# Weight tiles loaded as two DMAs of half the columns, each with its own semaphore

## The chip, the cores and the metric

The kernel runs on one core of one Trainium2 chip. The metric is the device time of one execution in microseconds (us), the median of several runs.

## What is computed

The reference runs one activation `x` of 256 tokens by 1024 features, all float32, through two blocks of two layers each. Every layer is a feed-forward part (FFN), a token mixer and a second FFN, each with a norm before or after it and a residual. Cut to what matters here:

```python
def swiglu(h, w_gate, w_up, w_down):          # D_MODEL 1024, D_FF 2816
    return (jax.nn.silu(h @ w_gate) * (h @ w_up)) @ w_down

for l in range(DEPTH):                        # first block, DEPTH = 2
    x = x + 0.5 * rmsnorm(swiglu(rmsnorm(x, ...), gate, up, down), ...)
    x = x + rmsnorm(hybrid_mixer(rmsnorm(x, ...), w_in, w_out, ...), ...)
    x = x + 0.5 * rmsnorm(swiglu(rmsnorm(x, ...), gate, up, down), ...)
...
for l in range(DEPTH):                        # second block: layer norms, and a
    mod = cond @ w_ada[l] + b_ada[l]          # modulation from the vector c
    ...                                       # FFN, token mixer, FFN again
```

So there are eight FFNs and four mixers. The weights, some 330 MB of gate, up, down, `w_in`, `w_out` tiles and the 72 MB of `w_ada`, are each read once from HBM.

## The kernel before

**Weight tiles and units.** Gate, up, down, `w_in` and `w_out` are laid out in HBM as tiles of 128 partitions by 2048 float32 columns, 1 MB, each partition's 8 KB in one piece. A tile goes by one DMA into one of four slots of `raw` in SBUF. A tile is worked off as two *units* of 1024 columns. For each unit ScalarE (ACT) copies the columns, rounded to fp32r, into `w_hi` (`hi_unit`, line 186), VectorE (DVE) subtracts that from `raw` and so makes the rest `w_lo` (`lo_unit`, line 192), and TensorE (PE) multiplies both parts with the two-part activation. `w_hi` and `w_lo` have three buffers.

**The semaphores of a unit.** `raw_in[slot]` counts the DMAs that landed in a slot (16 per DMA). `hi_unit` waits for it only at the first unit of a tile (`half == 0`), and always for `unit_done`, by which PE frees the buffer. `unit_hi` and `unit_lo` count finished splits; PE waits for both, and SyncE (SP) waits for `unit_lo` before it sends a new tile into a slot. `CREDIT` is a constant offset of `unit_lo` and `unit_done`.

**The FFN.** Eleven blocks (`NF`) of 256 hidden columns. In iteration i of the loop over 1 to 10 PE does two gate units, two up units (`wide_unit`, lines 225 and 230, each 8 matmuls of 512 columns and 8 of 256), and then the two down units of block i-1 (`row_unit`, lines 259 and 265, 8 matmuls and 4). Slot 0 holds gate, slot 1 up, slot 2 down. SP issues (`ffn_sp`, line 275) the gate tile as soon as the up tile before it has been split, and the up tile and the down tile together once the down tile before them has been split. In six of the eight FFNs eight of the iterations also carry a 1.5 MB chunk of `w_ada` on the same queue (line 1554). After the loop comes the **tail**: SP waits until every unit but the last two is split, issues the last down tile into slot 2, and ACT, DVE and PE do, in this order, `hi_unit`, `split_act` (line 330) and `hi_unit` on ACT; `lo_unit`, `rest_act` (line 369) and `lo_unit` on DVE; `row_unit` twice on PE. The last activation is put in `hT` here, and PE's first matmul of the tail waits for both its parts and for the first unit. Then the post norm reads the accumulators (DVE line 529 in the first block, line 555 in the second).

**The mixers.** `mixer_load` (line 592) sends the tiles of `w_in` and `w_out` into the four slots in turn, each when the tile four before it has been split; one tile of the first block's mixers is `w_small` with 160 columns, which is a single unit.

All order is written by hand: each engine's program is a list of instructions and waits.

Of the kernel before, what the change touches and what calls it, by code (L numbers as in the profile page):

```python
# [40 lines left out]
SLOTS = 4  # L41
UNIT = 1024
# [65 lines left out]
def build(nc, t, out):  # L108
    ctx = ExitStack()

    def sb(name, shape, dt=F32):
        return ctx.enter_context(nc.sbuf_tensor(name, shape, dt))

    def sem(name):
        return ctx.enter_context(nc.semaphore(name))
# [10 lines left out]
    raw = sb("raw", [P, SLOTS, KT * FB])  # L126
# [20 lines left out]
    settled = sem("settled")  # L147
    rows_in = [sem("rows_in0"), sem("rows_in1")]
    zero_set = sem("zero_set")
    raw_in = [sem(f"raw_in{i}") for i in range(SLOTS)]  # L150
    unit_hi, unit_lo = sem("unit_hi"), sem("unit_lo")
    unit_done = sem("unit_done")
    silu_done, act_ready = sem("silu_done"), sem("act_ready")
# [26 lines left out]

    def hi_unit(a, B, j, buf, slot, loads, half, width=UNIT):

        if half == 0:
            a.wait_ge(raw_in[slot], loads * 16)
        a.wait_ge(unit_done, B + (j - UBUF + 1 + CREDIT if not isinstance(j, tuple) else j[0] + (j[1] - UBUF + 1 + CREDIT)))
        nc.scalar.activation(w_hi[:, buf, 0:width], raw[:, slot, half * UNIT:half * UNIT + width],  # L186
                             ACT.Copy).then_inc(unit_hi, 1)
# [84 lines left out]

    def ffn_sp(sp, B, loads, l, wg, wu, wd, between=None):
        def load(slot, w, i):
            sp.dma_start(raw[:, slot, :], w[bass.ds(l, 1), i, :, :].rearrange("l i p n -> p (l i n)")).then_inc(
                raw_in[slot], 16)


        sp.wait_ge(unit_lo, B + (CREDIT - 6))
        load(0, wg, slice(0, 1))  # L280
        sp.wait_ge(unit_lo, B + (CREDIT - 4))
        load(1, wu, slice(0, 1))
        for first, end in FFN_LOOPS if between else ((1, NF),):
            with sp.Fori(first, end) as i:
                sp.wait_ge(unit_lo, B + i * 6 + (CREDIT - 4))
                load(0, wg, bass.ds(i, 1))
                sp.wait_ge(unit_lo, B + i * 6 + (CREDIT - 2))
                load(1, wu, bass.ds(i, 1))
                load(2, wd, bass.ds(i - 1, 1))
                if between and first == 1:  # L290
                    between(first_chunk)
                if between and first == 2:
                    between(i - 1)
        sp.wait_ge(unit_lo, B + (6 * NF - 2 + CREDIT))
        load(2, wd, slice(NF - 1, NF))
# [30 lines left out]
    def ffn_act(a, B, loads, f):  # L326
# [18 lines left out]
        for r in range(4):  # L345
            hi_unit(a, B, r if r >= UBUF - 1 else UBUF - 1, r % UBUF, r // 2, loads + 1, r % 2)
# [3 lines left out]
        with a.Fori(1, NF) as i:  # L350
            for r in range(2):
                hi_unit(a, B, (i * 6, r - 2), (r - 2) % UBUF, 0, loads + i + 1, r)
            split_act(f * NF + i - 1, B + i * 6 + (CREDIT - 2))
            for r in range(2, 4):
                hi_unit(a, B, (i * 6, r - 2), (r - 2) % UBUF, 1, loads + i + 1, r - 2)
            gate_copy(f * NF + i, B + i * 6 + CREDIT)
            hi_unit(a, B, (i * 6, 2), 2, 2, loads + i, 0)
            silu(f * NF + i)
            hi_unit(a, B, (i * 6, 3), 0, 2, loads + i, 1)
            up_copy(f * NF + i, B + i * 6 + (2 + CREDIT))  # L360
# [228 lines left out]
    def mixer_load(sp, B, ends, n, src, width=KT * FB):  # L589

        sp.wait_ge(unit_lo, B + (CREDIT + (ends[n - SLOTS] if n >= SLOTS else (-4, -2, 0, 0)[n])))
        sp.dma_start(raw[:, n % SLOTS, 0:width], src).then_inc(raw_in[n % SLOTS], 16)

    def mixer_units(ends, n):

# [164 lines left out]
    def mixer1_sp(sp, B, l):  # L760
        at = 0
        for n in range(IN1 + WO):
            if n == SMALL_AT:
                mixer_load(sp, B, ENDS1, n, t["w_small"][bass.ds(l, 1), :, :].rearrange("l p n -> p (l n)"), KT * SMALL)
            elif n < IN1:
                mixer_load(sp, B, ENDS1, n, t["w_in"][bass.ds(l, 1), at:at + 1, :, :].rearrange("l i p n -> p (l i n)"))
                at += 1
            else:
                mixer_load(sp, B, ENDS1, n,
                           t["w_out"][bass.ds(l, 1), n - IN1:n - IN1 + 1, :, :].rearrange("l i p n -> p (l i n)"))  # L770
# [747 lines left out]
    half = m2.take(TILES, 512)  # L1518
# [647 lines left out]
```

## Time and profile before

| | |
|---|---|
| median of 3 runs | 2555.84 us (2554.86 to 2558.20) |
| the profiled execution | 2557.87 us, of which its span 2556.1 us |
| PE busy | 2299.2 us, 90% of the span |
| DVE busy | 1635.9 us, 64% |
| ACT busy | 1146.8 us, 45% |
| DMA queue of SP | 444.40 MB, packets take 45.4% of 16 DMA engines' span |

The span is the time from the first to the last instruction in the profile; 1.8 us of the execution lie around it. A busy share is an average over the eight FFNs, the four mixers and the norms between them, which have different limits. The profile also gives, for any stretch, the clock that TensorE was granted (1.00 stands for 2.4 GHz, 0.50 for 1.2 GHz, and what lies between is a mix of the two within the stretch).

### The profile page before, as it was taken

The page shows a single profiled execution, that of the slowest core. Times are in us where ns is not written, and L with a number is a line of the kernel's source. Part 1 is how long each engine was busy: PE and PEld are TensorE (multiplying, and loading weights), DVE is VectorE, ACT ScalarE, POOL GpSimd, SP SyncE. Part 2 cuts the span into 40 slices and gives each one's busy share as a digit, 9 for nine tenths or more (in the row PEclk, how much of TensorE's full clock was granted, in tenths as well). Part 3 has the DMA queues.
Part 4 walks back from the last instruction along what each step waited for, and adds up shares of the span by engine and source line. Part 5 has one row for each costly group of instructions (what it writes and reads, how often), then busy time and mean ns, then how long its engine had stood idle before and what let it go on. Part 6 is the DMA issues. An engine that isn't in the chain of part 4 may idle for free. (4 is left out here: it accounts for less than half of the span.)

```text
span 2556.1 us, 36360 instructions
## 1 busy us (share of the span) xinstructions
PE 2299.2 (90%) x13308; PEld 2036.2 (80%) x13308; DVE 1635.9 (64%) x1802; ACT 1146.8 (45%) x1418; POOL 24.5 (1%) x14
## 2 busy tenths in 40 slices
PE   6998997799799989888998998967998998877996
PEld 5888897688688889777887887956887887866885
DVE  5775756577577557646765776556775665555655
ACT  4543533454455444335544553434553544443553
POOL 0000000000000000000000000000000000000000
PEclk9997997899899989889998998979998999978998
DMA  7763320276377432205755763513763444421442
GB/s 275 287 238 133 116 99 17 108 289 261 148 290 285 176 115 102 81 17 222 283 201 199 279 266 132 190 42 141 278 254 128 185 183 178 149 83 66 183 181 113
DMA packets 58954, 445.62 MB, mean 174 GB/s; under 512 B 6896, under 2 KB 7280, under 8 KB 8304
## 3 DMA queue, kind: packets, MB, share of 16 engines
q1 hardware_dynamic: 58864, 444.40, 45.4%
q8 instruction: 59, 0.97, 0.2%
q14 instruction: 31, 0.25, 0.0%
HBM read 443.33 MB, written 1.05 MB: 174 GB/s over the span
## 5 line engine op out<-in xcount | busy, mean ns | idle before, releaser
L192 DVE TENSOR_TENSOR w_lo<-raw,w_hi 128x1024 fp32r<-128x1024 f32 x670 | 811.0, 1222 | 406.6 <-ACT w_hi L186 405.6
L186 ACT ACTIVATE w_hi<-raw 128x1024 fp32r<-128x1024 f32 x670 | 702.2, 1053 | 449.4 <-PE ps L230 161.0
L225 PE MATMUL ps<-hT,w_hi 128*128 128x512 f32 x2816 | 704.7, 392 | 22.8 <-ACT w_hi L186 13.1
L225 PEld LDWEIGHTS ps<-hT,w_hi 128*128 128x128 f32 x2816 | 510.7, 189 | 123.3 <-ACT w_hi L186 18.5
L230 PEld LDWEIGHTS ps<-hT,w_lo 128*128 128x128 f32 x2816 | 384.1, 190 | 27.5
L230 PE MATMUL ps<-hT,w_lo 128*128 128x256 f32 x2816 | 392.6, 282 | 0.0
L259 PE MATMUL ps<-w_hi,act_hi 128*128 128x512 f32 x640 | 198.5, 391 | 0.0
L259 PE MATMUL ps<-w_hi,act_lo 128*128 128x512 f32 x640 | 197.6, 390 | 0.0
L265 PE MATMUL ps<-w_lo,act_hi 128*128 128x512 f32 x640 | 171.0, 389 | 0.0
L242 PE MATMUL ps<-w_hi,hT 128*128 128x256 f32 (+1 forms) x576 | 146.9, 291 | 4.7 <-DVE hT L506 4.7
L243 PE MATMUL ps<-w_hi,hT 128*128 128x256 f32 (+1 forms) x576 | 145.3, 288 | 0.0
L1568 DVE SCALAR_TENSOR_TENSOR arena<-arena,cond 128x3072 f32<-128x3072 f32 x42 | 143.4, 3413 | 0.0
L259 PEld LDWEIGHTS ps<-w_hi,act_lo 128*128 128x128 f32 x640 | 120.1, 188 | 26.2
L265 PEld LDWEIGHTS ps<-w_lo,act_hi 128*128 128x128 f32 x640 | 120.1, 188 | 24.9
L259 PE MATMUL ps<-w_hi,hT 128*128 128x512 f32 x384 | 110.8, 437 | 29.1 <-DVE hT L369 17.4
L259 PEld LDWEIGHTS ps<-w_hi,act_hi 128*128 128x128 f32 x640 | 115.1, 189 | 19.3
L452 PE MATMUL ps<-base,tok 128*128 128x128 f32 x192 | 44.0, 423 | 92.8 <-DVE tok L490 54.8
L380 DVE TENSOR_TENSOR hidden<-ps,arena 128x512 f32<-128x512 f32 x88 | 60.9, 692 | 103.0 <-ACT arena L335 103.0
L343 ACT ACTIVATE arena<-ps 128x512 f32<-128x512 f32 x88 | 52.8, 600 | 162.4 <-PE ps L230 162.4
L259 PEld LDWEIGHTS ps<-w_hi,hT 128*128 128x128 f32 x384 | 80.1, 212 | 51.6 <-DVE hT L435 13.3
L335 ACT ACTIVATE arena<-ps 128x512 f32<-128x512 f32 x88 | 52.6, 598 | 152.7 <-PE ps L230 152.7
L242 PEld LDWEIGHTS ps<-w_hi,hT 128*128 128x128 f32 x576 | 114.2, 198 | 7.4 <-DVE hT L506 5.5
(314 smaller groups left out, 2656.6 us busy)
## 6 DMA issues: line engine op xcount, KB each, us to landing
raw<-in_g SPq DMA_DIRECT2D x88, 1024.0 KB, 4.8
raw<-in_u SPq DMA_DIRECT2D x88, 1024.0 KB, 4.8
raw<-in_d SPq DMA_DIRECT2D x88, 1024.0 KB, 6.7
arena<-in_w_ada SPq DMA_DIRECT2D x48, 1536.0 KB, 7.5
raw<-in_w_in SPq DMA_DIRECT2D x54, 1024.0 KB, 4.8
raw<-in_w_out SPq DMA_DIRECT2D x16, 1024.0 KB, 4.8
rows<-in_rows SPq DMA_DIRECT2D x12, 1024.0 KB, 6.8
arena<-in_con SPq DMA_DIRECT2D x1, 1344.0 KB, 5.7
```

Source lines behind the costliest of these rows:

```text
L186: nc.scalar.activation(w_hi[:, buf, 0:width], raw[:, slot, half * UNIT:half * UNIT + width], ACT.Copy).then_inc(unit_hi, 1)
L192: nc.vector.tensor_tensor(w_lo[:, buf, 0:width], raw[:, slot, half * UNIT:half * UNIT + width], w_hi[:, buf, 0:width].bitcast(F32), ALU.su ...
L225: nc.tensor.matmul(o, h_[:, k, c], hT[:, :, 4 * half + k, :], start=(half == k == 0), stop=False)
L230: last = nc.tensor.matmul(ps[:, bank + s, 0:SEQ], l_[:, k, c], hT_hi[:, 4 * half + k, :], start=False, stop=(half == 1 and k == 3))
L242: nc.tensor.matmul(o, hT_hi[:, 4 * half + k, c], h_[:, k, :], start=(half == tile == k == 0), stop=False)
L243: nc.tensor.matmul(o, hT_lo[:, 4 * half + k, c], h_[:, k, :], start=False, stop=False)
L259: nc.tensor.matmul(ps[:, 2 * tile + half, :], part[:, c], w_hi[:, buf, half * 512:(half + 1) * 512], start=start and i == 0, stop=False)
L265: last = nc.tensor.matmul(ps[:, 2 * tile + half, :], left[0][:, c], w_lo[:, buf, half * 512:(half + 1) * 512], start=False, stop=stop)
L335: nc.scalar.activation(part, ps[:, 4:6, SEQ:512], ACT.Copy).then_inc(gate_part, 1)
L343: nc.scalar.activation(part, ps[:, 6:8, SEQ:512], ACT.Copy).then_inc(up_part, 1)
L380: nc.vector.tensor_tensor(out_, in_, part, ALU.add).then_inc(gate_sum, 1)
L1568: nc.vector.scalar_tensor_tensor(ada, ada_w, cond[:, bass.ds(k, 1)], ada, ALU.mult, ALU.add).then_inc(ada_acc, 1)
```

## The change

Every load of a weight tile is issued as two DMAs, the first for the left half of the columns, the second for the right half. Each half has its own semaphore per slot, and `hi_unit` now waits for the semaphore of its own half, in both units. The narrow unit of `w_small`, whose two halves are both read by the one unit, waits for both.

```diff
-    raw_in = [sem(f"raw_in{i}") for i in range(SLOTS)]
+    raw_in = [[sem(f"raw_in{i}{h}") for h in "ab"] for i in range(SLOTS)]
...
     def hi_unit(a, B, j, buf, slot, loads, half, width=UNIT):
 
-        if half == 0:
-            a.wait_ge(raw_in[slot], loads * 16)
+        a.wait_ge(raw_in[slot][half], loads * 16)
+        if width < UNIT:
+            a.wait_ge(raw_in[slot][1], loads * 16)
...
     def ffn_sp(sp, B, loads, l, wg, wu, wd, between=None):
         def load(slot, w, i):
-            sp.dma_start(raw[:, slot, :], w[bass.ds(l, 1), i, :, :].rearrange("l i p n -> p (l i n)")).then_inc(
-                raw_in[slot], 16)
+            for half in range(2):
+                c = slice(half * UNIT, (half + 1) * UNIT)
+                sp.dma_start(raw[:, slot, c], w[bass.ds(l, 1), i, :, c].rearrange("l i p n -> p (l i n)")).then_inc(
+                    raw_in[slot][half], 16)
...
     def mixer_load(sp, B, ends, n, src, width=KT * FB):
 
         sp.wait_ge(unit_lo, B + (CREDIT + (ends[n - SLOTS] if n >= SLOTS else (-4, -2, 0, 0)[n])))
-        sp.dma_start(raw[:, n % SLOTS, 0:width], src).then_inc(raw_in[n % SLOTS], 16)
+        for half in range(2):
+            c = slice(half * width // 2, (half + 1) * width // 2)
+            sp.dma_start(raw[:, n % SLOTS, c], src[:, c]).then_inc(raw_in[n % SLOTS][half], 16)
```

On ACT, in the FFN's tail, these are the rows before: the last down tile's two splits around `split_act`. The names are the tiles written and read, and in brackets the semaphores waited for.

```order
L184 ISA
L185 REGISTER_ALU [waits raw_in2]
L186 ACTIVATE w_hi<-raw 128x1024 [waits unit_done]
L328 REGISTER_ALU
L330 ACTIVATE hT<-hidden 128x512 [waits unit_done,act_ready]
L185 REGISTER_ALU
L186 ACTIVATE w_hi<-raw 128x1024 [waits unit_done]
```

And these in the changed kernel:

```order
L183 ISA
L186 REGISTER_ALU [waits raw_in2a]
L187 ACTIVATE w_hi<-raw 128x1024 [waits unit_done]
L331 REGISTER_ALU
L333 ACTIVATE hT<-hidden 128x512 [waits unit_done,act_ready]
L186 REGISTER_ALU [waits raw_in2b]
L187 ACTIVATE w_hi<-raw 128x1024 [waits unit_done]
```

The number and order of the instructions are the same; the second split's wait rides on a register instruction that was there before.

On SP, at the end of the loop and in the tail, before:

```order
L287 REGISTER_ALU
L275 DMA raw<-in_u 128x2048 [waits unit_lo]
L275 ISA
L275 DMA raw<-in_d 128x2048
L284 REGISTER_ALU
L284 COMPARE_AND_BRANCH
L294 REGISTER_ALU
L275 ISA [waits unit_lo]
L275 DMA raw<-in_d 128x2048
```

And in the changed kernel:

```order
L290 REGISTER_ALU
L278 DMA raw<-in_u 128x1024 [waits unit_lo]
L278 DMA raw<-in_u 128x1024
L278 ISA
L278 DMA raw<-in_d 128x1024
L278 ISA
L278 DMA raw<-in_d 128x1024
L287 REGISTER_ALU
L287 COMPARE_AND_BRANCH
L297 REGISTER_ALU
L278 ISA [waits unit_lo]
L278 DMA raw<-in_d 128x1024
L278 ISA
L278 DMA raw<-in_d 128x1024
```

Each DMA became two, one behind the other under the same wait; nothing else moved.

## Rows read from the trace of the kernel before

**Rows 1.** The page, part 1: busy us (share of the span) xinstructions.

```profile
PE 2299.2 (90%) x13308; PEld 2036.2 (80%) x13308; DVE 1635.9 (64%) x1802; ACT 1146.8 (45%) x1418; POOL 24.5 (1%) x14
```

**Rows 2.** Waits of ACT: us in total, times, longest us.

```profile
ACT w_hi L186 <- DMA raw<-in_d: 31.3, 8, 4.4
...
ACT w_hi L186 <- DMA raw<-in_u: 0.4, 1, 0.4
```

**Rows 3.** Timeline, last FFN's tail: start us, us, engine line op [idle before].

```profile
2523.61 0.34 SPq L275 DMA_DIRECT2D raw<-in_d  x1
...
2528.41 1.07 PE L265 MATMUL ps<-w_lo,act_hi 128*128 128x512 f32 x4
2528.43 1.06 ACT L186 ACTIVATE w_hi<-raw 128x1024 fp32r<-128x1024 f32 x1 [3.78 <-DMA raw<-in_d]
2529.40 0.61 ACT L330 ACTIVATE hT<-hidden 128x512 fp32r<-128x512 f32 x1
2529.52 1.23 DVE L192 TENSOR_TENSOR w_lo<-raw,w_hi 128x1024 fp32r<-128x1024 f32 x1 [3.29 <-ACT w_hi L186]
...
2530.67 0.68 DVE L369 TENSOR_TENSOR hT<-hidden,hT 128x512 fp32r<-128x512 f32 x1
...
2531.45 2.48 PE L259 MATMUL ps<-w_hi,hT 128*128 128x512 f32 x8 [1.97 <-DVE hT L369]
...
2538.85 2.35 DVE L555 TENSOR_TENSOR tok<-ps,arena 128x1024 f32<-128x1024 f32 x2 [6.37 <-PE ps L265]
```

**Rows 4.** Timeline, PE and DVE in the tails of the first and fifth FFN.

```profile
205.41 3.49 PE L259 MATMUL ps<-w_hi,hT 128*128 128x512 f32 x8 [2.73 <-DVE hT L369]
...
1558.52 2.08 PE L259 MATMUL ps<-w_hi,hT 128*128 128x512 f32 x8 [1.94 <-DVE hT L369]
...
1564.27 2.35 DVE L555 TENSOR_TENSOR tok<-ps,arena 128x1024 f32<-128x1024 f32 x2 [4.71 <-PE ps L265]
```

**Rows 5.** Windows: from:to us, engines' busy times, PEclk, DMA share, GB/s.

```profile
205.40:209.00 3.60, 3.59 (x10) 2.88 (x11) 0.91 (x1) 0.00 (x0) 0.00 (x0) 0.58 0.56 178
1558.50:1562.00 3.50, 3.48 (x15) 2.92 (x16) 1.06 (x1) 0.83 (x1) 0.00 (x0) 1.00 0.67 232
2531.40:2535.00 3.60, 3.55 (x11) 2.85 (x12) 1.08 (x1) 0.85 (x1) 0.00 (x0) 0.71 0.00 0
```

**Rows 6.** Timeline, PE at the start of the first FFN.

```profile
23.18 2.11 PE L225 MATMUL ps<-hT,w_hi 128*128 128x512 f32 x8 [1.59 <-DVE hT L506]
```

**Rows 7.** DMA issues by line: xcount, KB each, median us from issue to landing.

```profile
raw<-in_u SPq DMA_DIRECT2D x88, 1024.0 KB, 4.8
raw<-in_d SPq DMA_DIRECT2D x88, 1024.0 KB, 6.7
arena<-in_w_ada SPq DMA_DIRECT2D x48, 1536.0 KB, 7.5
...
x<-in_x SPq DMA_DIRECT2D x1, 1024.0 KB, 5.2
...
base<-in_con SPq DMA_DIRECT2D x1, 256.0 KB, 5.3
raw<-in_w_small SPq DMA_DIRECT2D x2, 80.0 KB, 1.8
```

**Rows 8.** Timeline of the queue of SP: the kernel's first two loads.

```profile
0.75 0.45 SPq L1885 DMA_DIRECT2D x<-in_x  x1
...
1.25 0.46 SPq L1886 DMA_DIRECT2D base<-in_con  x1
```

**Rows 9.** Timeline, one loop iteration of the last FFN, SP and ACT.

```profile
2407.31 0.33 SPq L275 DMA_DIRECT2D raw<-in_u  x1
...
2407.86 0.33 SPq L275 DMA_DIRECT2D raw<-in_d  x1
...
2413.76 1.04 ACT L186 ACTIVATE w_hi<-raw 128x1024 fp32r<-128x1024 f32 x1
...
2423.93 0.33 SPq L275 DMA_DIRECT2D raw<-in_u  x1
```

## The prediction, made before the changed kernel ran

> **What bounds the kernel now.** The page's first part shows PE busy for 90% of the span [rows 1], so time can only be won where PE stands idle or runs at a low clock. A load can matter only where a split waits for it. The waits of ACT, read next, say where that is: the split at line 186 waited for a down tile 8 times, 31.3 us in total, and once, for 0.4 us, for an up tile; it never waited for a gate tile or for a tile of the mixers [rows 2]. There are eight FFNs, and the 8 waits are the eight tails. Everywhere else the tile has landed before ACT wants it. One loop iteration shows the margin: an up tile issued at 2407.31 lands 4.8 us later [rows 7], at 2412.11, and its first split starts at 2413.76 [rows 9], 1.65 us after that. So the loops and the mixers are bound by PE, and only the tails by a load.
>
> The timeline of a tail gives the chain [rows 3]. SP issues the last down tile at 2523.61, and the first split starts when it has landed, at 2528.43, 4.82 us later. Then the activation's split (2529.40 to 2530.01) and, on DVE, `w_lo` (2529.52 to 2530.75) and the activation's rest at line 369 (2530.67 to 2531.35), and PE starts at 2531.45. From the landing to PE's start that is 3.02 us of fixed work. PE had finished its earlier matmuls at 2529.48 and stood idle for 1.97 us. The other tails are alike, PE idle for 1.94 to 2.73 us [rows 3, 4]; five more lie between the three shown.
>
> That idle time costs a second time. In the last tail it takes 7.40 us from PE's first matmul (2531.45) to the post norm's first read of the result (2538.85) [rows 3], in the fifth FFN 5.75 us (1558.52 to 1564.27) [rows 4], for the same instructions. The granted clock explains it: 0.71 in the last tail's first 3.6 us and 0.58 in the first's, but 1.00 in the fifth's [rows 5]; the eight matmuls at line 259 take 3.49 us in the first tail and 2.08 us in the fifth [rows 4]. In seven of the eight tails the clock falls to the 1.2 GHz level for some 3 us just after the gap. In the last tail that costs 7.40 - 5.75 = 1.65 us, in the first 3.49 - 2.08 = 1.41 us; of the six tails between them in the timeline the fifth loses nothing and the other five 1.62 to 1.66 us each. Together 1.65 + 1.41 + 5 x 1.64 = 11.3 us.
>
> **The change, part by part.** *The first half lands earlier.* This is the term that counts, and no row shows a load of 512 KB alone, so I bound it. An up tile lands 4.8 us after its issue; the down tile issued 0.55 us later lands 6.7 us after its own, which is 2.45 us after the up tile [rows 7, 9]. So 1 MB takes the queue 2.45 us, and 4.8 - 2.45 = 2.35 us are paid once. With the queue's rate alone, half a tile lands at 2.35 + 1.23 = 3.58 us, 1.22 us earlier than now. The other bound is the line between `w_small` (80 KB in 1.8 us) and the full tile (1024 KB in 4.8 us) [rows 7]: 1.8 + 432 x 3.0 / 944 = 3.17 us, 1.63 us earlier. I take the middle, rounded down: 1.4 us. The chain behind it is on ACT, DVE and PE and does not change; its other inputs are ready (the activation was, PE's buffer too, since ACT's one wait of 3.78 us ended at the DMA [rows 3]). PE is idle for at least 1.94 us, so the whole 1.4 us reaches it: 8 x 1.4 = **11.2 us**.
>
> *The second half* is issued some 0.4 us behind the first (0.33 us for the issue and a register instruction) and lands about when the tile lands now, at 4.8 to 5.2 us. It is wanted by the second split, which stands behind the first (landing at 3.4, plus 1.06) and behind the activation's split (0.61), at 5.1 us. Even if it is 0.3 us late, PE needs that unit only after the first unit's 2.8 us of matmuls. Cost nothing, hidden by PE's first unit.
>
> *The clock.* With 1.4 us less of idle time, PE's gap in the tails shrinks from 1.94-2.73 to 0.5-1.3 us. At the eight FFN starts PE stands idle for up to 1.59 us just before its first matmuls, and these then run at full speed: 2.11 us for 8, as in the tail that kept its clock [rows 4, 6]. So I expect the clock to hold in the tails, and **11.3 us** to come back. The bounds are 0 (it still falls in seven) and 11.3.
>
> *ACT's added waits*: no instruction is added, the wait for the second half rides on one that stood there. What is queued behind it is ACT's next split and the activation's, and PE behind them. In the loop the second half is wanted 2.2 us after the first, and the first had 1.65 us to spare: nothing. *SP's added issues*: a tile costs SP one more issue of 0.33 us. In the loop three tiles go in 16.62 us (2407.31 to 2423.93 [rows 9]), so SP has the time; the down tile, issued behind the up tile, comes some 0.4 us later and the `w_ada` chunk 0.7 us later, each long before use. *Twice as many and smaller pieces*: 4 KB instead of 8 KB per partition, strided in HBM. Near rows: `x`, in pieces of 4 KB, lands at 0.75 + 5.2 = 5.95, and `base`, 256 KB in strided pieces of 2 KB, at 1.25 + 5.3 = 6.55 [rows 7, 8]. That is 0.60 us for 256 KB, or 2.4 us per MB, no worse than the 2.45 of the 8 KB pieces. Nothing. The mixers gain nothing: no split there waits for a load.
>
> The profiled execution is 2557.87 us, its span 2556.1 and 1.8 us around it. From it the sum is 2557.9 - 11.2 - 11.3 = 2535.4. It stood 2.0 us above the median of the runs, so the forecast for the median is 2555.8 - 22.5 = **2533.3 us**.
>
> *A page against a row.* The rows put 2.35 us of fixed time in a load and 1.22 to 1.63 us into half of a tile's bytes [rows 7, 9]. The Trainium skill, "DMA: Bandwidth & Descriptors", section "Anatomy of one DMA — SWDGE (gpsimd) path", fits 2.0 us plus the bytes over 436e3; half a tile would by that land 1.2 us earlier, and the first term would be an estimated 9.6 us in place of 11.2.
>
> **The rivals.** *The clock still falls.* The smaller gap may not be small enough, or the falls may depend on more than the gap: 1.94 us of idle kept the clock and 1.97 lost it [rows 3, 4]. For it: that thin edge. Against: gaps of up to 1.59 us that lose nothing [rows 6]. Then only the landing counts: 2555.8 - 11.2 = 2544.6 us.
>
> *The first half does not come earlier*, because the two halves share the queue and finish together, so that the change doesn't do what it says. Against it: the up tile lands at 4.8 us although the down tile is queued 0.55 us behind it, so the queue works in order [rows 7, 9]. For it: two DMAs 0.4 us apart could overlap more than two 0.55 us apart. Then the first split starts as now or up to 0.4 us later: 2555.8 to 2559.
>
> *Slower: each DMA pays its fixed part in turn.* If two halves do not overlap, a tile holds the queue for 2 x 3.58 = 7.2 us. An iteration of 16.62 us brings three tiles, in 48 of the 80 iterations also a chunk of 1.5 MB (1.5 x 2.45 = 3.7 us) [rows 7, 9]. Then 3 x 7.2 = 21.5 us bind the loop, 4.9 us too long in all 80 and 3.7 more in the 48: 390 + 178, or some 3110 us with the tails' gain. It decides from (16.62 - 3.7) / 3 = 4.3 us per tile; the rows have 2.45. The Trainium skill, same page, section "Measured (HBM→SBUF, 128 partitions, SWDGE, issued from GpSimd)", has the rule behind this, to batch DMAs to 1 MiB or more; the trace's back-to-back loads speak against it here, since the second lands 2.45 us after the first.
>
> **How the numbers follow.** The forecast 0.62; the clock still falls 0.20; no earlier half 0.12; slower loops 0.04; the rest, 0.02, for a larger gain. The range takes in the first two: at the low end 8 x 1.63 + 11.3 = 24.3 us gained, and at the high end 8 x 1.22 = 9.8 us and no clock, 2531.5 to 2546.0. The kernel's clock falls in many other places too, each fall being worth about 1.6 us, and their number may shift with the timing; I add 3.5 to 4 us each side: 2528 to 2550. A measurement of this kernel can tell about 0.2% (5.1 us) from no change. Faster by more: the first two cases and the rest, less a little for an unlucky clock, 0.82. Same: 0.13. Slower: 0.05.
>
> **What would show it.** In the waits, the line of ACT on the down tile should fall from 31.3 us to about 31.3 - 11.2 = 20. In the tails the first split should start 3.2 to 3.6 us after the issue, PE's gap should be 0.5 to 1.3 us, and the time from PE's first matmul to the post norm 5.75 us, with a granted clock of 1.00. The loop should still take 16.62 us, and two tiles in a row still land 2.4 to 2.5 us apart. It is wrong if the first half lands at 4.5 us or later, if the clock in the tails is still near 0.6, or if ACT begins to wait for loads inside the loop.

## The result, and the profile after

The changed kernel takes 2540.81 us (median of 4 runs, 2537.62 to 2542.17) against 2556.35 us for the kernel before (4 runs): 15.5 us less, a ratio of 0.9937 with a 95% interval of 0.992 to 0.9954. Timed a second time it was 17.0 us less (2538.47 against 2555.50 us), a ratio of 0.9929 (0.9911 to 0.9946). The forecast was faster, by 22.5 us. The direction held; the size forecast was 7 us too large.

The page of the profiled execution (2542.17 us, span 2540.3), its engines, its queue and its loads, to be read beside [rows 1] and [rows 7]:

```profile
PE 2293.6 (90%) x13308; PEld 2032.6 (80%) x13308; DVE 1636.4 (64%) x1802; ACT 1146.3 (45%) x1418; POOL 24.5 (1%) x14
...
q1 hardware_dynamic: 107248, 444.42, 49.8%
...
raw<-in_g SPq DMA_DIRECT2D x176, 512.0 KB, 4.6
raw<-in_u SPq DMA_DIRECT2D x176, 512.0 KB, 4.7
raw<-in_d SPq DMA_DIRECT2D x176, 512.0 KB, 6.6
arena<-in_w_ada SPq DMA_DIRECT2D x48, 1536.0 KB, 9.1
```

The work is the same. The queue's packets take 49.8% of the span in place of 45.4%, and a chunk of `w_ada`, which stands behind the halves, lands 9.1 us after its issue, 7.5 before [rows 7]. So the halves are not free for the queue. The waits of ACT say whether that matters:

```profile
ACT w_hi L187 <- PE ps L231: 162.0, 168, 1.8
...
ACT w_hi L187 <- DMA raw<-in_d: 24.1, 8, 3.4
```

There are still exactly 8 waits for a down tile, the eight tails; those for other tiles are gone. But the 8 fell only from 31.3 us [rows 2] to 24.1, by 0.9 us each, where 1.4 was forecast. The last FFN's tail, which answers to [rows 3]:

```profile
2510.35 1.03 SPq L278 DMA_DIRECT2D raw<-in_d  x2
...
2514.27 1.06 ACT L187 ACTIVATE w_hi<-raw 128x1024 fp32r<-128x1024 f32 x1 [2.88 <-DMA raw<-in_d]
...
2515.15 1.07 PE L266 MATMUL ps<-w_lo,act_hi 128*128 128x512 f32 x4
...
2515.95 1.06 ACT L187 ACTIVATE w_hi<-raw 128x1024 fp32r<-128x1024 f32 x1
...
2517.30 2.06 PE L260 MATMUL ps<-w_hi,hT 128*128 128x512 f32 x8 [1.07 <-issue]
...
2523.02 2.36 DVE L558 TENSOR_TENSOR tok<-ps,arena 128x1024 f32<-128x1024 f32 x2 [4.69 <-PE ps L266]
```

The first split starts 3.92 us after the issue (4.82 before; 3.8 to 4.3 in all eight tails), PE's gap is 2517.30 - 2516.22 = 1.08 us (1.97 before), the 8 matmuls take 2.06 us (2.48), and from PE's first matmul to the post norm it is 5.72 us (7.40). The clock held. In windows of the last and the first tail, to be read beside [rows 5], the column PEclk stands at 1.00 where it was 0.71 and 0.58:

```profile
204.10:207.70 3.60, 3.56 (x16) 2.96 (x17) 0.94 (x1) 0.00 (x0) 0.00 (x0) 1.00 0.93 340
2517.30:2520.90 3.60, 3.60 (x16) 3.01 (x17) 1.03 (x1) 1.01 (x1) 0.00 (x0) 1.00 0.00 0
```

All eight tails are so. From the tile's issue to the post norm's first read, the eight tails took 120.8 us before and 102.9 us after: 17.9 us less, of which 11.2 are the clock (57.2 us from PE's first matmul to the post norm before, 46.0 after) and 6.7 the landing. (Measured by PE's gaps, 17.4 us in all before and 10.2 after, the landing gives 7.2, because in two of the tails the issue itself comes 0.1 and 0.4 us sooner, seen from PE's earlier work.) The spans differ by 15.8 us, so elsewhere the kernel was 2.1 us *longer*. Whether the halves cost that was the first open question; the second was why half a tile comes only 0.9 us earlier.

### The profile page after: what moved, and what is told of

It is laid out like the page before. It is cut to its first block and busy times, and to the rows that moved or that the text cites. A ratio compares the mean times of both kernels' runs of the same rounds, so it can differ in the third digit from the quotient of the medians.

```text
span 2540.3 us, 37230 instructions
## 1 busy us (share of the span) xinstructions
PE 2293.6 (90%) x13308; PEld 2032.6 (80%) x13308; DVE 1636.4 (64%) x1802; ACT 1146.3 (45%) x1418; POOL 24.5 (1%) x14
## 3 DMA queue, kind: packets, MB, share of 16 engines
q1 hardware_dynamic: 107248, 444.42, 49.8%
## 5 line engine op out<-in xcount | busy, mean ns | idle before, releaser
L226 PEld LDWEIGHTS ps<-hT,w_hi 128*128 128x128 f32 x2816 | 510.7, 189 | 122.9 <-ACT w_hi L187 18.4
L260 PE MATMUL ps<-w_hi,hT 128*128 128x512 f32 x384 | 103.0, 413 | 21.9 <-DVE hT L438 11.8
L243 PEld LDWEIGHTS ps<-w_hi,hT 128*128 128x128 f32 x576 | 115.1, 200 | 7.4 <-DVE hT L509 5.5
L244 PEld LDWEIGHTS ps<-w_hi,hT 128*128 128x128 f32 x576 | 115.2, 200 | 0.0
```

The lines of the kernel that those rows point to most:

```text
L226: nc.tensor.matmul(o, h_[:, k, c], hT[:, :, 4 * half + k, :], start=(half == k == 0), stop=False)
L243: nc.tensor.matmul(o, hT_hi[:, 4 * half + k, c], h_[:, k, :], start=(half == tile == k == 0), stop=False)
L244: nc.tensor.matmul(o, hT_lo[:, 4 * half + k, c], h_[:, k, :], start=False, stop=False)
L260: nc.tensor.matmul(ps[:, 2 * tile + half, :], part[:, c], w_hi[:, buf, half * 512:(half + 1) * 512], start=start and i == 0, stop=False)
```

## How the experiments are read

The kernel's time moves by several us between executions that are otherwise alike (the kernel before gave 2543 to 2561 us over all runs). The traces show where. I cut each trace at two points of each FFN that every kernel has: the start of the last product of gate and up on DVE, from which the tail's work hangs, and the post norm's first read. The sum of the eight pieces between them is "tails", the rest up to the last tail "between". "Tails" holds the clock's part and the change of PE's gaps, 11.2 + 7.2 = 18.4 us for the change. All in us, one profiled execution each:

| kernel | tails | between | time against before, with interval |
|---|---|---|---|
| before | 106.1 | 2432.8 | 1 |
| the change | 87.7 | 2435.4 | 0.9937 (0.992 to 0.9954) |
| the change, again | 87.4 | 2432.7 | 0.9929 (0.9911 to 0.9946) |
| halves in the tails alone | 87.8 | 2429.3 | 0.9945 (0.9923 to 0.9967) |
| halves everywhere but in the tails | 103.3 | 2435.0 | 1.0009 (0.9994 to 1.0024) |
| tails' gap filled on PE | 94.7 | 2430.9 | 0.9972 (0.9959 to 0.9985) |
| last down tile in slot 3 | 75.3 | 2432.8 | 0.9885 (0.9859 to 0.9912) |
| slot 3, again | 75.3 | 2437.6 | 0.988 (0.9865 to 0.9895) |
| one DMA of 4 KB pieces | 105.5 | 2431.2 | one execution, no interval: 2555.65 us |
| second half sent after the first | 85.4 | 2431.3 | one execution, no interval: 2535.87 us |
| each half in one piece of HBM | 82.6 | 2435.7 | one execution, no interval: 2537.42 us |
| the same, timed | 82.9 | 2426.0 | 0.9899 (0.9881 to 0.9917) |

"Tails" repeats within 0.3 us for a like kernel. "Between" runs from 2426 to 2438 with no order in it that the edits would give.

## Experiments: where the gain is made

**Halves in the tails alone.** The kernel before, with this in place of the last down load, and a wait for `tail_in` at the last split:

```diff
-        load(2, wd, slice(NF - 1, NF))
+        for half in range(2):
+            c = slice(half * UNIT, (half + 1) * UNIT)
+            sp.dma_start(raw[:, 2, c], wd[..., NF - 1:NF, :, c]...).then_inc(tail_in if half else raw_in[2], 16)
```

> The kernel before, with only the last down tile of each FFN loaded as two halves; every other tile goes by one DMA as before. Theory: the whole gain of the change (15.5 us) is made in the eight tails, where the traces show 17.9 us less from the tile's issue to the post norm, and the twice as many DMAs in the loops and mixers do nothing. Then about 2540.8 us, as the change, with the tail's first split starting 3.8 to 4.3 us after the issue. Rival: the small DMAs in loops and mixers cost the 2 us that are missing between 17.9 and 15.8; then about 2538.5 us.

Measured: 2537.59 us, ratio 0.9945. The eight halved loads of the tails bring what halving all of them brought. The waits of ACT are those of the change, 24.1 us there:

```profile
ACT w_hi L189 <- DMA raw<-in_d: 24.2, 8, 3.5
```

**The change again, and its complement.** The second kernel is the change with the tail's tile whole again:

```diff
+        sp.dma_start(raw[:, 2, :], wd[..., NF - 1:NF, :, :]...).then_inc(raw_in[2][0], 16)
...
         hi_unit(a, B, 6 * NF - 2, (6 * NF - 2) % UBUF, 2, loads + NF, 0)
+        a.sem_inc(raw_in[2][1], 16)
```

> The changed kernel again, beside the two that follow. Theory: 15 to 16 us under the kernel before, of which the tails' landing gives 6.6 and their clock the rest. Rival (the halves in loops and mixers cost time): it stays slower than the kernel with halves in the tails alone (5.5 permille under before in the job ahead) by 2 us or more.

> The changed kernel, but the last down tile of each FFN is again one DMA of 1 MB. Theory: the halves in loops and mixers are hidden by PE's work, both ways, so this is the kernel before: no difference above 0.1% (2 to 3 us). Rival: they cost about 2 us (the traces of before and after differ by 2.1 us in that sense outside the tails), a ratio of 1.001.

Measured: 0.9929 and 1.0009. The change is not behind the kernel that halves only the tails (0.9929 and 0.9945, intervals overlapping), and halves in all loops and mixers but not in the tails are no different from the kernel before; the interval leaves room for a cost of up to 0.24% and for none. The gain is made in the tails. The 2.1 us that were missing between the first two traces are within the scatter of "between" and I don't put them down to the DMAs.

## Experiments: the clock

**PE's gap filled.** The loads are those of before; PE does six matmuls of zeros in front of the tail:

```diff
+        pe.wait_ge(act_ready, f * NF + (NF + 1))
+        for _ in range(6):
+            nc.tensor.matmul(ps[:, 6, :], zero[:, 0:P], zero[:], start=True, stop=True)
         pe.wait_ge(act_split, f * NF + NF)
```

> The kernel before, loads unchanged, but PE does six matmuls of zeros (128 x 512, bf16, into a PSUM bank that is free there) between its last loop unit and the tail, about 1.8 us that fill most of its gap of 1.94 to 2.73 us. Theory: the clock falls in the tails because PE stands idle there; filled, it holds, each tail takes 5.75 us from PE's first useful matmul to the post norm, and the kernel gains 11.3 us: about 2545 us. Rival: the falls don't hang on the gap (or zeros don't count as work): still 7.4 us per tail, 2556 us.

Measured: 2546.05 us, ratio 0.9972. The last tail and its window, columns as above:

```profile
2516.86 1.06 ACT L186 ACTIVATE w_hi<-raw 128x1024 fp32r<-128x1024 f32 x1 [3.77 <-DMA raw<-in_d]
...
2517.98 1.24 PE L322 MATMUL ps<-zero 128*128 128x512 bf16 x5
...
2519.88 2.09 PE L259 MATMUL ps<-w_hi,hT 128*128 128x512 f32 x8 [0.66 <-issue]
...
2525.64 1.23 DVE L558 TENSOR_TENSOR tok<-ps,arena 128x1024 f32<-128x1024 f32 x1 [4.72 <-PE ps L265]
```

```profile
2519.50:2523.00 3.50, 3.12 (x14) 2.60 (x15) 1.41 (x2) 1.18 (x1) 0.00 (x0) 1.00 0.00 0
```

ACT still waits 3.77 us for the tile, PE's useful work starts as late as before, and yet each tail is 5.76 to 5.79 us from there to the post norm: the eight sum up to 11.4 us less than before. With nothing changed but what PE does in the gap, the clock's fall is gone, so the gap causes it. (The row of zeros has five of the six matmuls; one record is missing. They leave 0.57 to 1.36 us of idle time.) The timed gain is smaller than the trace's 11.4, 7 us (4 to 10). The next rows give a part of the reason: a kernel with a whole tile in the tail doesn't always lose seven tails. These are two tails of the kernel with halves everywhere but in the tails:

```profile
1561.36 3.65 PE L260 MATMUL ps<-w_hi,hT 128*128 128x512 f32 x8 [1.93 <-DVE hT L374]
...
2156.76 2.09 PE L260 MATMUL ps<-w_hi,hT 128*128 128x512 f32 x8 [1.93 <-DVE hT L374]
```

The same gap of 1.93 us lost the clock once and kept it once. In the three traces with a whole tile in the tail the clock fell in 7, 6 and 5 of 8 tails, all with gaps of 1.91 to 2.87 us; in the nine traces in which the gap is smaller or filled (at most 1.84 us) it fell in none of 72. The six gaps that kept the clock were 1.91 to 2.16 us long, among falls that begin at 1.93; what decides between them is not shown. On average 6 of 8 falls at 1.64 us, or 9.8 us, is my estimate of what the change gives back; it rests on one trace each of three kernels.

## Experiments: the landing

**One DMA of 4 KB pieces.** The host lays each tile out as two halves of 128 x 1024, and one DMA loads both:

```diff
-            sp.dma_start(raw[:, slot, :], w[bass.ds(l, 1), i, :, :].rearrange("l i p n -> p (l i n)")).then_inc(
-                raw_in[slot], 16)
+            sp.dma_start(raw[:, slot, :].rearrange("p (h n) -> p h n", h=2),
+                         w[bass.ds(l, 1), i, :, :, :].rearrange("l i h p n -> p (l i h) n")).then_inc(raw_in[slot], 16)
```

> The kernel before, one DMA per tile, but the weights lie in HBM as two halves of 128 x 1024, so that each DMA moves 256 pieces of 4 KB instead of 128 of 8 KB. It tells what made the halves land later than bounded (3.9 us instead of 3.2 to 3.6). Theory: the smaller pieces cost queue time. Then the tile lands at 5.1 to 5.4 us after its issue instead of 4.8, and an up and a down tile back to back land about 2.8 to 3.3 us apart. Rival: it is the second DMA, not the pieces: landing stays at 4.8 us, 2.45 us apart. The time moves little: 2556 to 2561 us.

Measured, DMA issues by line as in [rows 7]:

```profile
raw<-in_g SPq DMA_DIRECT2D x88, 1024.0 KB, 4.8
raw<-in_u SPq DMA_DIRECT2D x88, 1024.0 KB, 4.9
raw<-in_d SPq DMA_DIRECT2D x88, 1024.0 KB, 6.8
```

Up and down land 0.1 us later at most, 2.59 us apart in the iteration that I read (median of all 2.55; before 2.48). The theory of that run, that the smaller pieces as such cost the time, is out: they cost 0.1 us per tile.

**The second half sent after the first,** and **each half in one piece of HBM.** In the first, halves in the tails alone, SP waits for the first half before it sends the second:

```diff
+            if half:
+                sp.wait_ge(raw_in[2], (loads + NF) * 16)
```

The other is the change, with the host layout of the run above, each of the two DMAs reading its own 512 KB:

```diff
-                sp.dma_start(raw[:, slot, c], w[bass.ds(l, 1), i, :, c].rearrange("l i p n -> p (l i n)")).then_inc(
+                sp.dma_start(raw[:, slot, c], w[bass.ds(l, 1), i, half:half + 1, :, :].rearrange("l i h p n -> p (l i h n)")).then_inc(
```

> Halves in the tails alone, and SP issues the second half only when the first has landed, so that the first is alone on the queue. Theory A: the second half's transfer holds the first up; alone, the first lands 3.2 to 3.6 us after its issue, as was forecast from the queue's rate. Theory B: half a tile simply has more fixed time than the rate says; it still lands at 3.8 to 3.9 us. The second half lands at 7 to 8 us and its split is done at 9, in time for PE's second unit; so the kernel's time is that of halves in the tails alone, less up to 8 x 0.5 us if A holds.

> The changed kernel, but each half of a tile lies in HBM in one piece of 512 KB. It tells whether the strided reads or the second DMA make the queue slower for halves: in the change an up and a down tile back to back land 3.3 us apart (before: 2.45; one DMA with 4 KB pieces: 2.6). Theory: it is the second DMA, so still 3.2 to 3.4 us apart, the first half at 3.9 us. Rival: the 8 KB stride in HBM; then 2.5 to 2.7 us apart and the first half at 3.4 to 3.6 us. Time about 2538 to 2542 us either way.

Measured: the times from issue to landing (smallest, median, largest) of the tails' 16 halves, first for halves in the tails alone, then with the second half sent later:

```profile
DMA to landing us min/median/max: 3.8/4.3/5.3
```

```profile
DMA to landing us min/median/max: 3.5/3.7/4.4
```

These lines mix first and second halves. The first halves by themselves land at 3.8 to 4.1 us (median 3.9) with the second right behind, and at 3.5 to 3.9 us (median 3.6) alone; ACT's start moves by 0.3 us. Both theories had a part: the second half's transfer holds the first one up by 0.3 us, and alone it is still at the upper bound of what was forecast. In one piece of HBM, with the second half right behind, it is better still. The page of that kernel, against 4.6, 4.7 and 6.6 in the change, and its last tail:

```profile
raw<-in_g SPq DMA_DIRECT2D x176, 512.0 KB, 3.9
raw<-in_u SPq DMA_DIRECT2D x176, 512.0 KB, 4.0
raw<-in_d SPq DMA_DIRECT2D x176, 512.0 KB, 6.3
```

```profile
2506.16 1.03 SPq L278 DMA_DIRECT2D raw<-in_d  x2
...
2509.49 1.06 ACT L187 ACTIVATE w_hi<-raw 128x1024 fp32r<-128x1024 f32 x1 [2.29 <-DMA raw<-in_d]
...
2511.25 1.06 ACT L187 ACTIVATE w_hi<-raw 128x1024 fp32r<-128x1024 f32 x1 [0.18 <-DMA raw<-in_d]
```

The split starts 3.33 us after the issue, 1.5 us earlier than in the kernel before, inside the 3.17 to 3.58 us that the forecast had bounded. Here my stated theory (the second DMA is to blame, the first half stays at 3.9 us) fell and its rival held: the changed kernel reads 4 KB out of every 8 KB of HBM, and that is what makes its first half land 0.6 us later. What the rival got wrong is the pair: an up and a down tile in halves are still in only 8.3 us after the first issue (median of the iterations; 8.6 in the change, 7.3 before, 7.4 with one DMA of 4 KB pieces). So four DMAs in a row take about 1 us longer to land than two of twice the size. Nothing waits for that here, and its cause is open. The queue's own line tells the two effects apart, first for one DMA of 4 KB pieces, then for halves in one piece of HBM:

```profile
q1 hardware_dynamic: 101616, 444.40, 46.8%
```

```profile
q1 hardware_dynamic: 107248, 444.42, 46.9%
```

The change, with as many DMAs and packets as the second, has 49.8%. Its packets thus take more of the queue's time because of the stride, and not because the DMAs are twice as many.

**That kernel timed.**

> The changed kernel with each half in one piece of HBM again, now timed. In one look its first halves landed at 3.3 us instead of 3.9. Theory: that is 8 x 0.4 to 0.5 us more at PE (its gaps then 0.1 to 1.1 us), the clock having nothing more to give: 3 to 4 us under the changed kernel, some 19 to 20 us under the kernel before (ratio 0.9925). Rival: PE's earlier work or DVE's chain now ends last in some tails, and it is level with the change, 0.9935.

Measured: 2528.03 us (2526.40 to 2537.74, 5 runs), ratio 0.9899, 28.7 us under before, more than any term explains. The tails give 106.1 - 82.9 = 23.2 us, 4.8 more than the change's 18.4, where 3 to 4 were expected. The rest lies in "between": 2426.0 in its trace, 2435.7 in the earlier execution of the same program. The first-block mixer shows how two executions of one program differ, the earlier one first (windows; PEclk is the third number from the right):

```profile
880.00:1320.00 440.00, 396.23 (x2472) 359.93 (x2472) 292.06 (x374) 192.96 (x263) 7.47 (x3) 0.91 0.39 146
```

```profile
880.00:1320.00 440.00, 396.76 (x2512) 359.78 (x2513) 295.68 (x377) 195.74 (x265) 7.46 (x3) 0.93 0.39 146
```

The granted clock is 0.91 in one and 0.93 in the other, for the same instructions (the stages lie a few us apart): within the 440 us the granted clock was at its lower level in ten places, and in seven. Whole runs go the same way: the four of the five that took 2526 to 2530 us had a mean granted clock of 0.937 to 0.939, the one of 2537.74 us had 0.933. The kernel before had 0.937 in its shortest run (2543.23 us) and 0.929 in its longest (2560.78). Why four runs of five came out well here stays open: whether the new timing of the stages favours the good case, or the sample did.

## Experiment: a version that beats both

**The last down tile in slot 3.** The FFN leaves one slot of `raw` unused. This kernel sends the last down tile there, whole, at the FFN's start (the counts of landed loads for which ACT waits are changed to match, which is left out here):

```diff
+        sp.wait_ge(unit_lo, B + CREDIT)
+        sp.dma_start(raw[:, 3, :], wd[..., NF - 1:NF, :, :]...).then_inc(tail_in, 16)
...
-        sp.wait_ge(unit_lo, B + (6 * NF - 2 + CREDIT))
-        load(2, wd, slice(NF - 1, NF))
```

> The kernel before with whole tiles, but the last down tile goes into slot 3 of raw, which the FFN doesn't use, at the FFN's start, so that it has landed long before the tail. Theory: the tail's load is the only wait that the change acted on; with it gone PE's gaps (1.94 to 2.73 us, 17.4 us in all) vanish and the clock holds (11.3 us): 28.7 us gained, about 2527.7 us. Rival: another wait (the activation's split and its rest) takes over part of the gap, or the added load at the FFN's start delays its first units: 2532 to 2540 us.

> The last down tile whole, in slot 3, issued at the FFN's start, again: does the version hold that beats both? Theory: 26 to 30 us under the kernel before (ratio 0.989), and so 10 us or more under the change, since here no tail waits for a load at all. Rival: the first job's value was a lucky one; 22 to 24 us.

Measured: 2525.13 and 2525.92 us, ratios 0.9885 and 0.988. The last tail:

```profile
2499.39 0.63 ACT L332 ACTIVATE hT<-hidden 128x512 fp32r<-128x512 f32 x1 [0.68 <-DVE hidden L390]
...
2500.41 0.69 DVE L371 TENSOR_TENSOR hT<-hidden,hT 128x512 fp32r<-128x512 f32 x1
...
2501.53 1.07 PE L266 MATMUL ps<-w_lo,act_hi 128*128 128x512 f32 x4
2502.43 1.98 PE L260 MATMUL ps<-w_hi,hT 128*128 128x512 f32 x8
```

No split waits for a down tile, PE goes from its loop units into the tail without a gap, and its own work is the bound. The tails take 75.3 us, 12.4 less than with the change. Of the change's idea nothing is needed: the tile's arrival was late only because it was asked for late. The timed values are less far apart: 27.8 and 30.9 us under before, and the halves in one piece of HBM, with tails of 82.9 us, came to 28.7 in their one timing, with an interval that overlaps these. By the tails slot 3 is 7.6 us ahead of them; by time that isn't shown.

## Why the prediction was right in direction and 7 us too large

*Where the time could be won* was right: the eight tails, and nothing in loops or mixers. The complement run (1.0009) and the tails-alone run (0.9945) show it.

*The first half lands earlier* is the term that was mis-sized: 8 x 1.4 = 11.2 us forecast, 6.7 us in the traces, 0.84 us each (7.2 and 0.9 by PE's gaps). The bounds, 3.17 to 3.58 us, came from rows of loads that read HBM in whole rows, and hold for such halves (3.3 us measured). The changed kernel's halves are strided, and 3.9 us lies outside. The step that failed is the one that set the smaller, strided pieces at nothing from the row of `base` [rows 7, 8]. That row says nothing of the time to landing of a single load, since `base` stood behind `x`. The sign that hung on the same step failed too: an up and a down tile, which were to land 2.4 to 2.5 us apart, land 3.3 us apart. That is the price of twice as many DMAs and not of the pieces, for halves in one piece of HBM are 3.7 us apart and uncut tiles of 4 KB pieces 2.55 us (medians). The piece size was indeed nearly free (0.1 us). The stride cost 0.6 us, and the DMA right behind 0.3 us where the halves were strided; a half in one piece and alone was not run.

*The second half* landed a little later than I put it: 5.0 to 5.6 us after the tile's issue, not 4.8 to 5.2. It cost nothing, as argued, since PE wants that unit 2.8 us after its first.

*The clock* was right in kind and, for the profiled execution, in size: 11.2 us against 11.3, with the gaps at 1.0 to 1.8 us (0.5 to 1.3 forecast). But I took one trace's seven falls for the median execution's. Over three traces it is six, 9.8 us, so the forecast of the median was 1.5 us too large there.

*The loop* kept its 16.62 us, and *the rival with slower loops* was wrong by its condition: the queue needs some 0.6 us more per tile, far from the 4.3 us per tile at which it would bind. The rule on which it leaned is to batch DMAs to 1 MiB or more (the Trainium skill, "DMA: Bandwidth & Descriptors", section "Measured (HBM→SBUF, 128 partitions, SWDGE, issued from GpSimd)"). In this case's traces a price of smaller DMAs shows in the landing of four in a row, 8.3 us in place of the 7.4 that two uncut tiles of equal pieces take. In the queue's share it doesn't: 46.9% and 46.8%. It cost nothing here, where the queue has room. *The clock still falls* and *no earlier half* did not happen.

Of 22.5 us forecast, the landing gave 6.7 in place of 11.2 and the clock about 9.8 in place of 11.3, together 16.5; the measured 15.5 and 17.0 (the second timing) lie on either side.

## What to carry to other kernels

Before a load is cut into pieces to get the first piece sooner, look whether it can be asked for sooner: a free slot gave here 28 to 31 us where the strided halves gave 15 to 17. If it must be cut, cut it so that each piece is whole in HBM (that gave 4.8 us more in the eight tails, and 28.7 us in all in its one timing), and only where something waits for it. And when PE stands idle for about 2 us in an otherwise dense stretch, price the gap twice, once for itself and once for the clock behind it; filling it with matmuls of zeros wins the second part back.

## What the runs showed of the hardware

- 512 KB of 4 KB rows landed 3.3 us after their issue when they lie in one piece of HBM, 3.9 us when they are every other 4 KB, both with a second such load right behind; 3.6 us strided and alone; 1 MB took 4.8 us in pieces of 8 KB and 4.8 to 4.9 us in pieces of 4 KB.
- The queue's packets took 45.4% of the span for whole tiles, 46.8% in pieces of 4 KB by one DMA, 46.9% in halves of one piece of HBM each, 49.8% in strided halves.
- Four loads of 512 KB in a row landed 8.3 us (each in one piece) to 8.6 us (strided) after the first issue, two of 1 MB 7.3 us, or 7.4 in pieces of 4 KB (medians).
- The clock fell to its 1.2 GHz level behind PE gaps of 1.91 to 2.87 us in 18 of 24 tails, each fall costing about 1.6 us, and in none of 72 tails with a gap of up to 1.84 us or a filled one. The same gap, 1.93 us, went either way. Six matmuls of zeros in the gap kept the clock up in all 8 tails.
- Executions of one program differ by 10 us and more in this kernel; the two compared above differ in the clock granted to the mixer, and the longer runs have the lower mean clock. So an interval from several runs is needed even for a change of 0.5%.
